# Moving columns and their products taken in lines of 16, in the order 0, 8, 1, 9, 2, 10 and so on

## The reference, cut to what matters

```python
proj = h @ w_in                       # Mamba-2: the part xbc
u = h @ w_up                          # both feed-forward networks: 1024 x 5632
q = h @ peer_wq                       # the experts' queries
act = gelu(h @ peer_u.T)              # the experts' first matrix: all 16384 of them
```

## Time and profile before

| | before |
|---|---|
| median of three runs | 1770.12 us |
| lowest and highest run | 1768.28, 1774.59 us |
| profiled execution, first to last instruction | 1774.7 us |
| the run nearest to it, of the three | 1774.59 us |
| PE busy | 1710.5 us, 96% |
| PE weight loads busy | 1606.4 us, 91% |
| DVE, ACT, POOL busy | 59%, 47%, 51% |
| moved by DMA | 310.79 MB, 175 GB/s |

### The profile page before, as it was taken

How to read it: one execution, slowest core, us unless ns; L and a number is a source line. 1 busy time by engine, 2 the same in 40 slices (tenths; PEclk the granted TensorE clock), 3 DMA queues, 4 the chain that set the end, 5 groups by cost and what they waited for, 6 DMA issues and landing times. The chain is left out here.

```text
span 1774.7 us, 34933 instructions
## 1 busy us (share of the span) xinstructions
PE 1710.5 (96%) x12583; PEld 1606.4 (91%) x12583; DVE 1044.9 (59%) x2198; ACT 826.9 (47%) x1147; POOL 900.8 (51%) x275
## 2 busy tenths in 40 slices
PE   8899799999999999999998999999999999999997
PEld 8889799999997999999678999999999978888886
DVE  7857654345344554344885891745555377777776
ACT  4578343334547433345435544644444443333332
POOL 4676468887682378876205588776666500000000
PEclk9999999999998999999988999999999999999999
DMA  5443335555452245554202466665555687777774
GB/s 212 143 144 118 113 126 190 190 188 192 143 190 72 72 167 190 188 183 160 93 1 84 164 234 236 210 205 177 178 177 177 216 266 240 240 241 243 239 242 160
DMA packets 77453, 310.79 MB, mean 175 GB/s; under 512 B 8768, under 2 KB 10304, under 8 KB 60736
## 3 DMA queue, kind: packets, MB, share of 16 engines
q1 hardware_dynamic: 75024, 306.14, 51.3%
q10 hardware_dynamic: 2352, 3.59, 0.6%
HBM read 290.82 MB, written 18.87 MB: 175 GB/s over the span
## 5 line engine op out<-in xcount | busy, mean ns | idle before, releaser
L759 POOL TENSOR_TENSOR lo<-raw,hi 128x2048 fp32r<-128x2048 f32 x127 | 584.3, 4610 | 378.1 <-ACT hi L584 306.0
L362 PE MATMUL ps<-xc,hi 128*128 128x256 f32 x1912 | 544.3, 285 | 5.7 <-DVE ps L2052 3.3
L363 PE MATMUL ps<-xcl,hi 128*128 128x256 f32 x1912 | 536.3, 280 | 0.0
L364 PE MATMUL ps<-xc,lo 128*128 128x256 f32 x1912 | 536.1, 280 | 0.0
L362 PEld LDWEIGHTS ps<-xc,hi 128*128 128x128 f32 x1912 | 362.6, 190 | 8.6 <-issue 6.9
L798 POOL TENSOR_TENSOR lo<-raw,hi 128x1024 fp32r<-128x1024 f32 x128 | 304.7, 2404 | 128.8 <-ACT hi L1767 128.7
L363 PEld LDWEIGHTS ps<-xcl,hi 128*128 128x128 f32 x1912 | 364.3, 191 | 0.1
L1767 ACT ACTIVATE hi<-raw 128x1024 fp32r<-128x1024 f32 x256 | 264.9, 1058 | 211.3 <-PE ps L364 199.0
L364 PEld LDWEIGHTS ps<-xc,lo 128*128 128x128 f32 x1912 | 360.6, 189 | 0.0
L2472 DVE TENSOR_TENSOR lo<-raw,hi 128x1024 fp32r<-128x1024 f32 x128 | 156.4, 1222 | 81.1 <-ACT hi L1767 81.0
L362 PE MATMUL ps<-hi,wgh 128*128 128x512 f32 x512 | 199.4, 389 | 1.8 <-DVE wgl L2483 1.8
(11 more groups left out here) (497 smaller groups left out, 3426.6 us busy)
## 6 DMA issues: line engine op xcount, KB each, us to landing
raw<-in_w_u SPq DMA_DIRECT2D x128, 512.0 KB, 4.3
raw<-in_w_v SPq DMA_DIRECT2D x128, 512.0 KB, 4.2
raw<-in_w_up SPq DMA_DIRECT2D x44, 1024.0 KB, 4.8
raw<-in_w_down SPq DMA_DIRECT2D x22, 1024.0 KB, 4.7
raw<-in_w_fox SPq DMA_DIRECT2D x16, 1024.0 KB, 5.0
act_save<-act_out SPq DMA_DIRECT2D x64, 256.0 KB, 2.1
act_in<-act_save SPq DMA_DIRECT2D x64, 256.0 KB, 3.2
raw<-in_w_xbc SPq DMA_DIRECT2D x12, 1024.0 KB, 5.0
```

Of the source, the lines that this page charges most:

```text
L362: pe.matmul(o, ah, bh, start=start, stop=False)
L363: pe.matmul(o, ah, bl, start=False, stop=False)
L364: return pe.matmul(o, al, bh, start=False, stop=stop)
L759: return g.tensor_tensor(lo[slot][:], raw[slot][:], hi[slot][:].bitcast(F32), ALU.subtract)
```

## The change

`by_line` gives the same 256 columns in another order: the access pattern has the dimensions 8, 2 and 16, with steps of 16, 128 and 1 columns. So columns 0 to 15 come first, then 128 to 143, then 16 to 31, then 144 to 159, and so on. It is laid on the moving operand and on the output alike, so each product lands in its own column of PSUM, and what other engines read there does not change. Each engine's program has as many instructions as before, in the same order (5737 of them on PE's list of both kernels, 128x256 of the touched matmuls written as 128x8x2x16). The `conv` units with 272 columns keep the plain order, as do all other users of `three`.

```diff
+    def by_line(ap):
+
+        return ap.rearrange("p (b c d) -> p c b d", b=2, c=8)
+
     def pe_a(pe, s, outs, x=None, ready=None, middle=None):
 
         xh_, xl_ = x or (xc[:], xcl[:])
@@ -373,8 +377,9 @@
                     pe.wait_ge(x_ready, ready + k // 2 + 1)
                 if middle is not None and f == 1 and k == 4:
                     middle()
-                m = three(pe, outs[f], wh[:, k, f * P:(f + 1) * P], wl[:, k, f * P:(f + 1) * P],
-                          xh_[:, k, :], xl_[:, k, :], k == 0, k == KC - 1)
+                order = by_line if outs[f].shape[1] == SEQ else lambda ap: ap
+                m = three(pe, order(outs[f]), wh[:, k, f * P:(f + 1) * P], wl[:, k, f * P:(f + 1) * P],
+                          order(xh_[:, k, :]), order(xl_[:, k, :]), k == 0, k == KC - 1)
         m.then_inc(unit_used, 1)
 
     def pe_b(pe, s, outs, width=256, x=None, ready=None, middle=None):
@@ -1334,8 +1339,8 @@
                 if f == 0 and (not isinstance(m, int) or m >= 2):
                     pe.wait_ge(a_gelu, m - 1)
                 for k in range(KC):
-                    mm = three(pe, ps[:, s, f * SEQ:(f + 1) * SEQ], wh[:, k, :], wl[:, k, :],
-                               xc[:, k, :], xcl[:, k, :], k == 0, k == KC - 1)
+                    mm = three(pe, by_line(ps[:, s, f * SEQ:(f + 1) * SEQ]), wh[:, k, :], wl[:, k, :],
+                               by_line(xc[:, k, :]), by_line(xcl[:, k, :]), k == 0, k == KC - 1)
                 mm.then_inc(e_used, 1)
```

## The result

| | before | after |
|---|---|---|
| median of the runs beside each other | 1769.20 us | 1789.22 us |
| lowest and highest of these four runs | 1766.83 to 1774.59 | 1787.66 to 1789.75 |
| ratio, 95% interval | | 1.0101, 1.0071 to 1.0132 |
| profiled span | 1774.7 us | 1787.2 us |

The change makes the kernel 1.0% slower, where 1.1% faster was forecast. The gap between the two profiles is 12.5 us and not 20, because the profiled execution of before is one of its longer ones: in 25 runs of it beside the first experiments it took 1759.13 to 1777.71 us, a width of 19 us, while the four runs of the changed kernel lie within 2.1 us. That width turns out to be part of the answer.

A forecast was written before the change was run, and what follows sets the result against it. PE (TensorE) alone was taken as the bound. 1774.7 - 20 + 0.9 gave about 1755.6 us, 19 us less; against the median 1770.1 that is 1751, stated as 1750 since up to 10 us more was open. Range 1738 to 1792.

The forecast's parts named there:

- "slower": Rival: each jump costs array time at the 5904 matmuls, 0.42 ns a jump, giving 1787 or 1807 us; chance 0.24.
- PE alone sets the pace; 5904 matmuls by a difference in pitch: In feed-forward and plain expert stretches PE is the bound; every term is touched matmuls times a change in start-to-start time.
- The gain of 20 us if all come to the lower level: All touched matmuls at 113.3 ns: 21.5 us, less 1.4 us for those in the first two groups already low.
- The two levels are the moving read and the weight load in each other's way: Touched matmuls start 117.8 or 113.3 ns apart, because moving read and next weight load hold each other up in memory.
- In the new order they never meet: For touched matmuls, both streams walk on together, 64 bytes apart, and never clash if they begin together.
- The jump between lines: Each touched matmul has 15 jumps in its read and 15 in its write; cost taken as nothing.
- the only row that jumps: Trace row of a bf16 matmul whose read jumps back three times, with no resolvable cost, under 1 ns each.
- The bounds from both sides (0 to 585 us): Cost of jumps over 5904 matmuls: from below nothing, from above 15 by 6.6 ns each, 585 us.
- The write that jumps: Jumping write of products to PSUM: no row in the trace; a skill rule on non-contiguous access spoke against the change.
- How much is at the lower level: Shares already low: some 300 in feed-forward and plain expert halves, every other gate half, half of xbc and queries.
- The `down` matmuls keep 118 ns: Untouched `down` matmuls of the feed-forward networks were to stay at about 118 ns in the changed profile.
- PE would wait 1 to 2 us at the lists: At L1350 PE waits for DVE's lists, which PE's faster pace can't shorten; 0.9 us of the gain is lost.

The follow-up runs named there:

- 25 runs: The kernel before, unchanged, run 25 times beside the first experiments: 1759.13 to 1777.71 us.
- the first experiments: Follow-up kernels, not listed one by one in the text; the kernel before, run beside them, took 1759.13 to 1777.71 us.
- Read alone: Changed kernel with the new order on the moving read only, products written in plain order: 1789.62 us, ratio 1.0113.
- write alone: Changed kernel with the new order on the written products only, moving columns read in plain order: 1769.94 us, ratio 1.0007.
- lines64: Changed kernel with read and write in four lines of 64 columns in place of 16 lines of 16: 1767.48 us, ratio 0.9989.

## Why the prediction was wrong, point by point

The forecast was 1750 us and 19 us less; measured were 1789.22 and 20 us more. That 1789 still lies inside the stated range, 1738 to 1792, is owed to the rival "slower", for which its upper end was put there, and not to the forecast.

- *PE alone sets the pace; 5904 matmuls by a difference in pitch.* Right for the direction: no new wait sets the pace. But the sum went by the pitch alone, and of the 19.7 us that the touched matmuls lost by it 7 came back, among others in shorter waits and in untouched matmuls at another level.
- *The gain of 20 us if all come to the lower level.* Its size was right: 116.7 ns on average before, less 113.3, is 20.0 us over 5904. It was never reached, because no matmul in lines of 16 came to 113.3.
- *The two levels are the moving read and the weight load in each other's way.* As far as it was tested, right: the plain pitch moved when only the slots of the weights moved, and when only `xc` moved, and it doesn't ask whether POOL or ACT works. The Trainium skill's "TensorE: Matmul & The Clock Gate", Step-by-step, has a load take nothing from a running matmul; here 113.5 and 118.5 ns for the same products with their weights 64 bytes further speak against it, and the measurement decides. What meets where was not seen. The working behind it was wrong in one place: it took 113.3 - 106.7 = 6.6 ns as what the change from one matmul to the next costs at most. Matmuls of 512 columns are 13.3 ns over their 213.3, twice as much, so in plain order this excess goes with the columns and not with the change of matmul.
- *In the new order they never meet.* The pitch in lines is free of the places: 120.0 ns at every one tried. That fits, but it is not shown that nothing clashes any more: a slower read might only hide it, and 120.0 is also what the plain order takes at its worst place.
- ***The jump between lines: "I take nothing, the value of the only row that jumps".*** This is the step that failed. Read alone and write alone show that the jumping read holds the loss. The 15 jumps measured 6.7 ns a matmul over the lower level, to which the forecast went, 0.44 ns a jump, or 39.6 us over 5904 where the sum has 0; that turned 20 us of gain into 19.7 of loss. The row it leaned on the earlier trace rows was a bf16 read with three jumps; the kernel with three jumps here (lines64) also shows nothing. From three jumps of another kind of operand nothing followed for fifteen. The bounds from both sides (0 to 585 us) held it, and the rival worked out the very case: one column's time a jump on top of 113.3 ns, "119.6 and the time ... 1787". It came out at 120.0 and 1789. All of "slower" stood at 0.24. That the number came so close is in part luck: the price a jump differs between the orders tried, and why a line costs what it does stays open.
- *The write that jumps.* The doubt was about the write, for which there was no row, and the read was thought to be covered. It was the other way round. The Trainium skill's "PSUM — Partial Sum Buffer", Specifications (TRN2), where any access that isn't contiguous slows matmuls significantly, is not borne out for lines of 16: write alone gave a ratio of 1.0007.
- *How much is at the lower level.* The forecast took the share of one profile for a constant. With the same code whole loops are at 113.3 or at 117.8 ns. In the profile before the lower level was rare in the feed-forward networks and the plain expert part (7 to 12% of their steps); the median of its runs is 5 us below that profile. The change takes the lower level away from all touched matmuls, so against the median it costs 20 us and against that profile 12.5.
- *The `down` matmuls keep 118 ns.* Wrong: 115.6 on average, 2.3 us back over both networks.
- *PE would wait 1 to 2 us at the lists.* Wrong with the sign of the rest: PE came later and did not wait.

## What to carry to other kernels

Measure the pitch from start to start before changing anything about a matmul: here the busy times of 280 and 284 ns said almost nothing, and counts in windows of equal length said everything. When such a change removes one cost and may bring another, a microscopic term must be measured on the same kind of operand with the same number of repeats; a single row that shows "no cost" for three jumps bounds fifteen of them only as loosely as its rounding does. And a kernel whose runs are 19 us apart at one clock may have levels of its own that no edit sets; look for them in the runs and in two profiles before pricing an edit from one. Compare the work's own pace with the end too: here 19.7 us of slower matmuls showed as 12.5.

## What the hardware showed that was not expected

- Rounded float32 matmuls, each with its own weight load, take 17 columns' time for 16 columns in plain order even at the lower level (113.3 ns for 256, 226.7 for 512, at a clock of 1.00), while a bf16 matmul of 512 columns was followed after 0.21 us.
- Lines of 16 in the order of this change take 18 for 16: 120.0 and 240.0 ns. So does the plain order of 256 columns where weights and moving columns start at the same place above a multiple of 256 bytes (120.0 ns). Steps of 64 columns in the 512-column matmul cost about half of that extra.
- Moving reads of 512 columns that start 32 bytes off a multiple of 64 took 233.3 ns for 226.7. Whether the start itself or the distance to the weights does it was not told apart.
- With the same instructions, a feed-forward network of 33 units ran throughout at 117.8 ns or throughout at 113.3, 190.7 or 184.3 us. What throws it to the one or the other stays open: no experiment set it on purpose.
